# Low parts of the lead's expert blocks made by GpSimd from a copy in SBUF, with a recast selection and an earlier end of the gate steps

## The chip, the cores and the metric

The kernel runs on one core of a Trainium2 chip. The metric is the device time of one execution in microseconds (us), and the profile is one execution taken by the hardware profiler. The core's engines are TensorE (PE, its weight loads PEld), VectorE (DVE), ScalarE (ACT), GpSimd (POOL) and SyncE (SP, which here only issues DMAs). Each runs its own instructions in order and waits for others by semaphores.

## The reference

A block of a transformer with 512 tokens and a model width of 1024: attention and an mLSTM side by side, then a PEER feed-forward. Only the PEER part is touched:

```python
def block(ht):                      # 64 tokens; h: 512 x 1024 in all
    q = (ht @ w_q).reshape(T, PEER_HEADS, 2, PEER_HALF)
    s1 = jnp.einsum('thd,hkd->thk', q[:, :, 0], keys1)
    s2 = jnp.einsum('thd,hkd->thk', q[:, :, 1], keys2)
    v1, i1 = lax.top_k(s1, PEER_TOPK)           # 16 of 128, 8 heads
    v2, i2 = lax.top_k(s2, PEER_TOPK)
    cand = (v1[..., :, None] + v2[..., None, :]).reshape(T, PEER_HEADS, 256)
    cidx = (i1[..., :, None] * PEER_KEYS + i2[..., None, :]).reshape(T, PEER_HEADS, 256)
    top, pos = lax.top_k(cand, PEER_TOPK)
    eidx = jnp.take_along_axis(cidx, pos, axis=-1)
    gate = jax.nn.softmax(top, axis=-1)
    act = gelu(jnp.einsum('thkd,td->thk', u[eidx], ht)) * gate
    return jnp.einsum('thk,thkd->td', act, v[eidx])
```

`u` and `v` have 16384 experts of 1024 numbers each.

## The kernel before

`mix_block` and `query_block` make the attention part and the queries. `peer_block`, which runs from 462.5 us on, is what the change touches. It treats the first 192 tokens and the other 320 differently. For the first 192 it gathers the chosen experts' rows (384 gathers of 128 rows, `pool.indirect_dma_start`, L1428) and DVE takes each with a dot product (`take_row`, L1683) or a scaled addition. For the 320 it computes all 16384 experts densely, in 128 blocks of 128 experts: PE transposes a block of `u`, multiplies it with the tokens, ACT applies the gelu, DVE multiplies with a table of gates that is zero where an expert wasn't chosen, and PE multiplies with the block of `v`.

Products are kept near full precision by splitting an operand in a high part `H` (rounded by ACT) and a low part `L` (what is left), three products in place of one.

**The lead** is the first 56 blocks (`LEAD`). In it only the scores are made and stored to `gelu_table` in DRAM, because the gates don't exist yet. In the same stretch DVE selects the 16 experts of each token and head, for four tiles of 128 tokens one after the other, and PE, DVE and ACT build the gate table in 80 steps (`gates`, `hot_rows`, `stage_gates`): DVE writes one-hot rows, PE multiplies them, ACT copies the result out, SP stores every fifth step's 1280 KB to `gate_table`. A lead block `it` on PE is: transpose block `it+1` to PSUM (`lead_turn`, L1528), 16 matmuls with `H` (L1543), two matmuls that subtract `H` of block `it+1` from its transpose in PSUM (`lead_less`, L1536), 8 matmuls with `L` (L1547), then the block's gate steps (L1555). ACT copies the transpose to `H` (`lead_high`, L1439) and, after L1536, what is left in PSUM to `L` (`lead_low`, L1444).

**What sets the order.** `SEL_AT` says at which block the selection of each of the four tiles must have ended: there DVE ends the softmax (`settle`) and PE turns the choice (`turn_choice`, L1565). The 80 steps are spread over the blocks between these (`gate_steps`), the gathered rows over all turns (`rows_by_turn`; 40 of the 384 in the lead). On DVE, selection code calls `beside(us, cap)`, which counts an estimated clock and puts a lead block's DVE work (`lead_block`: settle, one-hot rows, gathered rows) into the stream when the clock reaches the block's due time (`PE_BLOCK` and `PE_STEP` per block) and the block is before `cap`. After the last selection all remaining lead blocks follow in order. POOL runs only the gathers, six ahead of DVE (`RG`).

**After the lead** come 72 turns with a transpose, scores and values each, then 56 turns with values alone. The seam between lead and turns: SP waits for the last stores of the gate table, loads the first blocks of `v` and then the table's first parts (`load_g`), and DVE's first product with the gates (L1831) waits for these.

Names: `ring` holds loaded blocks of `u`, `peer_psum` is PSUM, `s_all` is a pool of SBUF that holds one-hot rows, selection scratch and later `v`; `s_in` holds candidates during the selection; `stage` holds parts of the gate table; `hT` and `more_rows` the gathered rows.

## Time and profile before

| | us |
|---|---|
| median of 3 runs | 1682.94 (1679.9 to 1685.92) |
| the profiled execution | 1675.21 |
| its span, first to last instruction | 1673.3 |
| PE busy | 1553.4 |
| DVE busy | 1407.6 |
| ACT busy | 618.5 |
| POOL busy | 497.2 |

The profiled execution is 7.7 us shorter than the median of the runs. Where a sum is made against the trace, its result is carried over to the median by the difference that it finds. In the trace the lead lasts from 462.5 us to 840 us, the seam to about 866 us, the 72 turns to 1439 us.

### The profile page before, as it was taken

Reading aid. Unit: us, or ns where it says so; the run is one execution under the profiler, and the core shown is the slowest. Engines: PE = TensorE matmul, PEld = TensorE weight load, DVE = VectorE, ACT = ScalarE, POOL = GpSimd, SP = SyncE. Lnnn points to the kernel's source line nnn. Section 1 sums busy time; section 2 is a strip of 40 time slices with the busy share of each in tenths; the row PEclk is TensorE's granted clock in tenths of the full one; section 3 lists DMA queues with packets and bytes.
Section 4 is the critical chain, followed back from the end, with each engine's and each line's share of the span. In section 5 each row is a group of like instructions: output and inputs, shape, how many; then the busy total and the mean of one; then the engine's idle time right before and its main releaser. Section 6 shows DMA issues by size and latency. Waiting matters only on the chain.

```text
span 1673.3 us, 23249 instructions
## 1 busy us (share of the span) xinstructions
PE 1553.4 (93%) x8386; PEld 1301.7 (78%) x8386; DVE 1407.6 (84%) x3000; ACT 618.5 (37%) x987; POOL 497.2 (30%) x424
## 2 busy tenths in 40 slices
PE   3999988969999689999959999999999999999996
PEld 2454544458899589999959999999999999888884
DVE  5867756649999996859959999999999999988887
ACT  1101423242155345555523333333333333334433
POOL 2000000033201111112235556555555555433330
PEclk8999899979999899999979999999999999999998
DMA  9563021042136556777999999999999999999992
GB/s 354 186 241 144 13 101 51 0 122 87 69 124 220 163 165 203 252 240 255 308 357 381 406 394 398 411 406 391 410 400 400 409 393 402 373 387 378 395 371 108
DMA packets 173425, 454.65 MB, mean 272 GB/s; under 512 B 13768, under 2 KB 72256, under 8 KB 171264
## 3 DMA queue, kind: packets, MB, share of 16 engines
q1 hardware_dynamic: 113152, 234.72, 38.8%
q0 software_dynamic: 59152, 216.07, 33.9%
q10 hardware_dynamic: 1008, 2.38, 0.4%
q8 instruction: 67, 1.10, 0.3%
q14 instruction: 46, 0.38, 0.1%
HBM read 420.58 MB, written 32.24 MB: 271 GB/s over the span
## 4 chain that ended last, share of the span: by engine, by line
PE 59%; DVE 11%; DMA 1%; ACT 1%; issue 1%; DVEq 0%; POOL 0%; ACTq 0%; SPq 0%; POOLq 0%
PE peer_psum L1543 14%; PE peer_psum L1603 7%; PE peer_psum L1614 7%; PE peer_psum L1610 7%; PE peer_psum L1547 7%; PE peer_psum L1555 4%; PE peer_psum L1590 4%; PE peer_psum L1607 4%; PE peer_psum L1616 4%; DVE s_all L1778 2%; DVE s_in L1783 2%; DVE s_all L1781 2%; PE peer_psum L1528 1%; PE peer_psum L1536 1%; DMA stage<-gate_table 1%
## 5 line engine op out<-in xcount | busy, mean ns | idle before, releaser
L1543 PE MATMUL peer_psum<-hH,hi_slots 128*128 128x320 f32 x1024 | 309.3, 316 | 16.9 <-ACT hi_slots L1498 15.4
L1543 PE MATMUL peer_psum<-hL,hi_slots 128*128 128x320 f32 x1024 | 304.0, 310 | 0.0
L1428 POOL DMA_INDIRECT hT<-in_peer_u,eidx x128 | 154.8, 1209 | 326.3 <-DVE dots L1683 277.2
L1464 ACT ACTIVATE hi_slots<-s_all 128x1024 fp32r<-128x1024 f32 x128 | 136.0, 1062 | 206.2 <-PE peer_psum L1616 203.9
L1543 PEld LDWEIGHTS peer_psum<-hH,hi_slots 128*128 128x128 f32 x1024 | 194.2, 190 | 21.9 <-issue 17.8
L1543 PEld LDWEIGHTS peer_psum<-hL,hi_slots 128*128 128x128 f32 x1024 | 194.2, 190 | 2.5
L1428 POOL DMA_INDIRECT hT<-in_peer_v,eidx x128 | 139.0, 1086 | 177.2 <-DVE s_all L1692 166.4
L1812 DVE TENSOR_TENSOR lo_slots<-s_all,hi_slots 128x1024 fp32r<-128x1024 f32 x128 | 156.4, 1222 | 22.9 <-ACT hi_slots L1464 22.9
L1547 PE MATMUL peer_psum<-hH,lo_slots 128*128 128x320 f32 x1024 | 171.7, 310 | 0.0
L1692 DVE SCALAR_TENSOR_TENSOR s_all<-hT,coef,s_all 128x1024 f32<-128x1024 f32 x126 | 161.2, 1279 | 2.5 <-DMA hT<-in_peer_v,eidx 2.1
L1547 PEld LDWEIGHTS peer_psum<-hH,lo_slots 128*128 128x128 f32 x1024 | 158.4, 189 | 4.8
L1603 PE MATMUL peer_psum<-hi_slots,a_hi_lo 128*128 128x512 f32 x512 | 146.7, 408 | 0.0
L1614 PE MATMUL peer_psum<-lo_slots,a_hi_lo 128*128 128x512 f32 x512 | 140.2, 394 | 0.0
L1610 PE MATMUL peer_psum<-hi_slots,a_hi_lo 128*128 128x512 f32 x512 | 139.5, 393 | 0.0
L1452 ACT ACTIVATE s_all<-peer_psum 128x320 f32<-128x320 f32 x128 | 56.0, 437 | 188.3 <-PE peer_psum L1547 182.5
L1610 PEld LDWEIGHTS peer_psum<-hi_slots,a_hi_lo 128*128 128x128 f32 x512 | 99.1, 194 | 20.1
L1614 PEld LDWEIGHTS peer_psum<-lo_slots,a_hi_lo 128*128 128x128 f32 x512 | 98.8, 193 | 20.5
L1495 ACT ACTIVATE a_hi_lo<-s_all 128x320 fp32r<-128x320 f32 x128 | 63.2, 494 | 120.7 <-DVE s_all L1831 120.7
L1428 POOL DMA_INDIRECT more_rows<-in_peer_u,eidx x64 | 72.0, 1126 | 117.9 <-DVE dots L1683 113.1
L1683 DVE CUSTOM_DVE_ANT_0 hT<-hT,h_rows 128x1024 f32<-128x1024 f32 x86 | 104.5, 1219 | 2.2 <-DMA hT<-in_peer_u,eidx 2.0
L1193 POOL TENSOR_TENSOR wqL<-wq,wqH 128x2048 fp32r<-128x2048 f32 x8 | 36.8, 4595 | 233.6 <-ACT wqH L1165 233.6
L1603 PEld LDWEIGHTS peer_psum<-hi_slots,a_hi_lo 128*128 128x128 f32 x512 | 94.1, 195 | 14.9
(305 smaller groups left out, 3042.9 us busy)
## 6 DMA issues: line engine op xcount, KB each, us to landing
ring<-in_peer_u SPq DMA_DIRECT2D x128, 512.0 KB, 7.5
s_all<-in_peer_v SPq DMA_DIRECT2D x128, 512.0 KB, 6.9
gate_table<-stage SPq DMA_DIRECT2D x16, 1280.0 KB, 7.3
stage<-gate_table SPq DMA_DIRECT2D x16, 1280.0 KB, 11.4
x_sb<-in_w_mod POOLq DMA_DIRECT2D x7, 2048.0 KB, 8.7
slab<-in_w_mod SPq DMA_DIRECT2D x5, 2048.0 KB, 15.3
gelu_table<-s_all SPq DMA_DIRECT2D x56, 160.0 KB, 1.9
s_in<-gelu_table SPq DMA_DIRECT2D x56, 160.0 KB, 6.8
```

Of the source, the lines that this page charges most:

```text
L1428: pool.indirect_dma_start(rows_of(j), None, A[table][0], bass.IndirectOffsetOnAxis(eidx[:, k:k + 1], 0)).then_inc(rows_in[j % RG], 16)
L1464: func(H[:, slot_of(w), :], vb[:, w % RING, :], ACT.Copy).then_inc(v_hi, 1)
L1543: mm(ps[:, bank, 0:TD], H[:, b, c * P:(c + 1) * P], h[:, c, T0:T], start=(c == 0 and h is hH), stop=False)
L1547: last = mm(ps[:, bank, 0:TD], L[:, b, c * P:(c + 1) * P], hH[:, c, T0:T], start=False, stop=(c == DC - 1))
L1555: last = mm(ps[:, 6 + m % 2, :].rearrange("p (i t) -> p t i", t=GT)[:, k, :], onehot[:, m % NHOT, k, 0, :], onehot[:, m % NHOT, k, 1, :], ...
L1590: last = tr(ps[:, 6 + (n + half) % 2, c * P:(c + 1) * P], ub[:, n % RING, (4 * half + c) * P:(4 * half + c + 1) * P], ident[:])
L1603: mm(y_bank(g, h), aH[:, NB + g * P:NB + (g + 1) * P], H[:, s, h * 512:(h + 1) * 512], start=first, stop=False)
L1610: mm(y_bank(g, h), aL[:, NB + g * P:NB + (g + 1) * P], H[:, s, h * 512:(h + 1) * 512], start=False, stop=False)
L1614: mm(y_bank(g, h), aH[:, NB + g * P:NB + (g + 1) * P], L[:, s, h * 512:(h + 1) * 512], start=False, stop=final)
L1683: v.tensor_tensor_reduce(out=rows_of(j), in0=rows_of(j), in1=(h_rows if j < K else keep["h_rows_b"])[:], scale=1.0, scalar=0.0, op0=ALU.mu ...
L1692: v.scalar_tensor_tensor(out=y0[:, i, :], in0=rows_of(j), scalar=c, in1=y0[:, i, :], op0=ALU.mult, op1=ALU.add).then_inc(row_done, 1)
L1812: v.tensor_tensor(L[:, s, :], vb[:, w % RING, :], H[:, s, :].bitcast(F32), ALU.subtract).then_inc(v_lo, 1)
```

## The change

- **PE** no longer subtracts. `lead_less` and the constant `minus_one` are gone.
- **ACT** copies the transpose to a new SBUF tile `whole` (one buffer of 128x1024) where it made `L` before. The copy of block `n` waits for GpSimd's subtraction of block `n-1`.
- **POOL** computes `L = whole - H` for each of the 56 lead blocks. The gathers, which POOL issued as early as it could, now stand between the subtractions at places fixed by `ROWS_BY`: six ahead of block 12, five ahead of block 26, then one or two at a block.
- **DVE's selection** adds values and indices in one instruction (tile `pairs`, 16 lists at once) over 11 rectangles, finds the largest of all 8 heads in one pass, and looks up the first 8 of the 16 chosen among the first 20 candidates only. Three groups of three instructions take the place of four.
- **The plan**: `SEL_AT` goes from 10, 20, 32, 45 to 12, 26, 32, 39; the gate steps end at block 50 (`G_END`) in place of 55; of the 40 gathered rows 14 are taken up to block 39 and 26 after (24 and 16 before); DVE's planned clock starts at 11 us.
- **The seam**: SP loads the first part of the gate table and the first four blocks of `v` at lead block 52, in place of after the lead.

```diff
-SEL_AT = {0: 10, 1: 20, 2: 32, 3: 45}
-ROWS_LEAD, ROWS_TAIL = (24, 16), 62
+SEL_AT = {0: 12, 1: 26, 2: 32, 3: 39}
+G_END = LEAD - 6
+DVE_BEHIND = 11.0
+ROWS_LEAD, ROWS_TAIL = (14, 26), 62
...
-    ends = {1: SEL_AT[2], 2: SEL_AT[3], 3: LEAD - 1}
+    ends = {1: SEL_AT[2], 2: SEL_AT[3], 3: G_END}
...
+ROWS_BY = [0 if it < SEL_AT[0] else EIDX_B_AT if it < SEL_AT[1] else RG + sum(ROWS_AT[i] for i in range(it - 2)) for it in range(LEAD)]
...
-RECTS = [(0, 1, 16), (1, 1, 8), (2, 1, 5), (3, 1, 4), (4, 1, 3), (5, 3, 2), (8, 8, 1)]
+RECTS = [(0, 1, 0, 8), (1, 1, 0, 4), (2, 2, 0, 2), (4, 4, 0, 1),
+         (0, 1, 8, 8), (1, 1, 4, 4), (2, 1, 2, 3), (3, 1, 2, 2), (4, 1, 1, 2), (5, 3, 1, 1), (8, 8, 0, 1)]
+FIRST = sum(nr * nb for r, nr, b0, nb in RECTS[:4])
...
+        whole = sb("whole", [P, D])
...
-            sp.wait_ge(g_full, GSTEPS)
-            for w in range(RING):
-                load_v(w)
-            for i in range(2):
-                sp.wait_ge(g_stored[i], 16 * (NTB // 2))
-            for i in range(2):
-                load_g(i)
+                if it == G_END + 2:
+                    for i in range(2):
+                        sp.wait_ge(g_stored[i], 16 * (NTB // 2))
+                    load_g(0)
+                    sp.wait_ge(g_full, GSTEPS)
+                    for w in range(RING):
+                        load_v(w)
+
+            load_g(1)
...
+            issued = 0
+            for n in range(LEAD):
+                b = n % 2
+                while issued < ROWS_BY[n]:
+                    gather(issued)
+                    issued += 1
+                pool.wait_ge(u_copied, n + 1)
+                nc.gpsimd.tensor_tensor(L[:, b, :], whole[:], H[:, b, :].bitcast(F32), ALU.subtract).then_inc(u_low, 1)
+            for j in range(issued, NROWS):
+                gather(j)
...
                 func(H[:, n % 2, :], uT_of(n % 2), ACT.Copy).then_inc(u_high, 1)
-
-            def lead_low(n):
-
-                act.wait_ge(u_less, n + 1)
-                func(L[:, n % 2, :], uT_of(n % 2), ACT.Copy).then_inc(u_low, 1)
+                if n:
+                    act.wait_ge(u_low, n)
+                func(whole[:], uT_of(n % 2), ACT.Copy).then_inc(u_copied, 1)
...
                 if n >= 2:
-                    pe.wait_ge(u_low, n - 1)
+                    pe.wait_ge(u_copied, n - 1)
...
-            def lead_less(n):
-
-                pe.wait_ge(u_high, n + 1)
-                for i in range(2):
-                    last = mm(ps[:, 2 * (n % 2) + i, :], minus_one[:], H[:, n % 2, i * 512:(i + 1) * 512],
-                              start=False, stop=True, skip_group_check=True)
-                last.then_inc(u_less, 1)
...
-            clock, due, blk = 0.0, 0.0, 0
+            clock, due, blk = DVE_BEHIND, 0.0, 0
...
-                for h in range(0, PH, 4):
-                    largest(v, step, [(top[:, t, h + i, :], pos[:, h + i, :], cv[:, h + i, :], work[:, i, :]) for i in range(4)])
-                    beside(4.6, cap)
+                largest(v, step, [(top[:, t, h, :], pos[:, h, :], cv[:, h, :], work[:, h, :]) for h in range(PH)])
+                beside(6.6, cap)
                 step(v.tensor_copy(posf, pos[:]))
-                for h in range(0, PH, 2):
...
+                for h, nh, k, n in ((0, PH, 0, FIRST), (0, 4, 8, NCAND), (4, 4, 8, NCAND)):
+                    hit, us = hit_of(nh, n), 0.18 + nh * 8 * n * 1.04e-3
```

POOL's stream in the lead, before: nothing but gathers after the last subtraction of the query stage (`wqL`).

```order
L1193 TENSOR_TENSOR wqL<-wq,wqH 128x2048 x8
L1412 IOTA iota_i 128x128
L1428 DMA hT<-in_peer_u,eidx 128x1024 x4
L1428 DMA more_rows<-in_peer_u,eidx 128x1024 x2
L1418 DMA eidx<-chosen_u 64x64
```

And after, the first 29 subtractions (`lo_slots` is `L`, `hi_slots` is `H`):

```order
L1447 TENSOR_TENSOR lo_slots<-whole,hi_slots 128x1024 x12
L1437 DMA hT<-in_peer_u,eidx 128x1024 x4
L1437 DMA more_rows<-in_peer_u,eidx 128x1024 x2
L1447 TENSOR_TENSOR lo_slots<-whole,hi_slots 128x1024 x14
L1427 DMA eidx<-chosen_u 64x64
L1437 DMA hT<-in_peer_u,eidx 128x1024 x4
L1437 DMA more_rows<-in_peer_u,eidx 128x1024
L1447 TENSOR_TENSOR lo_slots<-whole,hi_slots 128x1024 x2
```

The gathers have moved behind subtractions, and the subtractions of blocks 12 and 26 behind six and five gathers.

DVE's look-up of a tile's chosen experts, before (each of these groups of three stands four times):

```order
L1775 CAST s_in<-top_pos 128x128
L1778 TENSOR_TENSOR s_all<-iota,s_in 128x1600
L1781 TENSOR_TENSOR s_all<-s_all,s_in 128x1600
L1783 TENSOR_REDUCE s_in<-s_all 128x32
L1778 TENSOR_TENSOR s_all<-iota,s_in 128x1600
```

And after (the second group stands twice):

```order
L1777 CAST s_in<-top_pos 128x128
L1781 TENSOR_TENSOR s_all<-iota,s_in 128x1280
L1783 TENSOR_TENSOR s_all<-s_all,s_in 128x1280
L1785 TENSOR_REDUCE s_in<-s_all 128x8x8
L1781 TENSOR_TENSOR s_all<-iota,s_in 128x1600
L1783 TENSOR_TENSOR s_all<-s_all,s_in 128x1600
L1785 TENSOR_REDUCE s_in<-s_all 128x4x8
```

Three groups, the first of 1280 elements, stand for four of 1600.

SP at the seam, before (the last store of the gate table, then `v`, then both parts of the table):

```order
L1374 DMA gelu_table<-s_all 128x320
L1379 DMA gate_table<-stage 128x16x160
L1363 DMA s_all<-in_peer_v 128x1024 x4
L1366 DMA stage<-gate_table 128x2560 x2
L1360 DMA ring<-in_peer_u 128x1024 x2
```

And after, from the last store of the gate table at block 50 on:

```order
L1385 DMA gate_table<-stage 128x16x160
L1366 DMA ring<-in_peer_u 128x1024
L1380 DMA gelu_table<-s_all 128x320
L1372 DMA stage<-gate_table 128x2560
L1369 DMA s_all<-in_peer_v 128x1024 x4
L1366 DMA ring<-in_peer_u 128x1024
```

The first part of the table and four blocks of `v` are now asked for before the last three lead blocks' loads.

## Rows read from the trace of the kernel before

**Rows 1.** Windows: stretch, length, busy time per engine, granted clock, DMA share, GB/s.
```profile
462.40:565.00 102.60, 101.02 (x707) 98.72 (x708) 99.26 (x361) 57.29 (x69) 10.45 (x11) 1.00 0.55 179
565.00:640.00 75.00, 53.30 (x359) 50.10 (x357) 73.39 (x186) 27.70 (x36) 12.27 (x9) 0.89 0.49 157
...
840.00:880.00 40.00, 22.80 (x128) 21.11 (x129) 21.71 (x37) 8.88 (x16) 12.74 (x12) 0.79 0.99 362
880.00:1430.00 550.00, 549.51 (x3245) 501.08 (x3244) 528.30 (x746) 207.69 (x340) 308.06 (x266) 1.00 1.02 399
```
**Rows 2.** Timeline of PE in the lead: start, duration, line, operation, idle before.
```profile
488.31 0.62 PE L1536 MATMUL peer_psum<-hi_slots,minus_one 128*128 128x512 f32 x2
488.77 1.34 PE L1547 MATMUL peer_psum<-hH,lo_slots 128*128 128x320 f32 x8
...
493.63 1.34 PE L1547 MATMUL peer_psum<-hH,lo_slots 128*128 128x320 f32 x8
...
640.23 1.34 PE L1547 MATMUL peer_psum<-hH,lo_slots 128*128 128x320 f32 x8
...
645.98 1.32 PE L1547 MATMUL peer_psum<-hH,lo_slots 128*128 128x320 f32 x8
```
**Rows 3.** Timeline of DVE, selection of the first tile.
```profile
473.88 0.29 DVE L1758 CAST idxf<-idx 128x256 f32<-128x256 uint32 x1
...
483.86 1.82 DVE L1778 TENSOR_TENSOR s_all<-iota,s_in 128x1600 f32<-128x1600 f32 x1
485.72 1.82 DVE L1781 TENSOR_TENSOR s_all<-s_all,s_in 128x1600 f32<-128x1600 f32 x1
487.58 1.82 DVE L1783 TENSOR_REDUCE s_in<-s_all 128x32 f32<-128x1600 f32 x1
...
506.70 0.29 DVE L1758 CAST idxf<-idx 128x256 f32<-128x256 uint32 x1
```
**Rows 4.** Timeline of DVE: a gate step, a gathered row, the next step.
```profile
670.98 0.68 DVE L1719 TENSOR_TENSOR s_all<-iota,selT 128x512 f32<-128x512 f32 x1
671.58 1.11 DVE L1723 TENSOR_SCALAR s_all<-iota,selT 128x128 f32<-128x128 f32 x4
672.61 1.22 DVE L1683 CUSTOM_DVE_ANT_0 hT<-hT,h_rows 128x1024 f32<-128x1024 f32 x1
...
673.75 0.68 DVE L1719 TENSOR_TENSOR s_all<-iota,selT 128x512 f32<-128x512 f32 x1
```
**Rows 5.** Waits of PE, 462 to 880 us: total, times, longest.
```profile
PE peer_psum L1565 <- DVE gate_b L1704: 16.3, 1, 16.3
```
**Rows 6.** Groups by line: busy, mean ns, idle before.
```profile
L1444 ACT ACTIVATE lo_slots<-peer_psum 128x1024 fp32r<-128x1024 f32 x56 | 57.5, 1026 | 95.7 <-PE peer_psum L1536 95.7
L1193 POOL TENSOR_TENSOR wqL<-wq,wqH 128x2048 fp32r<-128x2048 f32 x8 | 36.8, 4595 | 233.6 <-ACT wqH L1165 233.6
```
**Rows 7.** Single lines' instructions: count, ns min/median/max, first and last start in us.
```profile
L787 DVE TENSOR_SCALAR mod_sum<-slab,cols x5: 486/487/646, 20.7 to 179.2; 128x512 f32<-128x512 f32 x5
...
L789 DVE SCALAR_TENSOR_TENSOR mod_sum<-slab,cols,mod_sum x35: 751/752/1024, 21.2 to 184.4; 128x512 f32<-128x512 f32 x35
...
L379 POOL TENSOR_SCALAR_AFFINE_SELECT x_sb<-x_sb x4: 629/818/1118, 165.6 to 169.6; 128x512 f32<-128x512 f32 x4
...
L1428 POOL DMA_INDIRECT hT<-in_peer_u,eidx x128: 936/946/2547, 506.7 to 1156.4; - x128
```
**Rows 8.** Timeline of the seam: the last gate steps, then who waits for what.
```profile
837.78 2.18 PE L1555 MATMUL peer_psum<-s_all 128*128 128x128 f32 x17
...
861.56 0.49 DVE L1831 TENSOR_TENSOR s_all<-s_all,stage 128x320 f32<-128x320 f32 x1 [13.20 <-DMA stage<-gate_table]
...
863.14 0.61 PE L1543 MATMUL peer_psum<-hH,hi_slots 128*128 128x320 f32 x1 [15.39 <-ACT hi_slots L1498]
```
**Rows 9.** DMA issues: count, KB each, median us to landing.
```profile
gate_table<-stage SPq DMA_DIRECT2D x16, 1280.0 KB, 7.3
stage<-gate_table SPq DMA_DIRECT2D x16, 1280.0 KB, 11.4
```

More of the change, by code:

```diff
@@ L1312, in peer_block @@
         iota = sb("iota", [P, P])
-        minus_one = sb("minus_one", [P, P], F32R)
         stat = sb("y_stat", [P, 5, 8])
@@ L1412, in _, with gather @@
             nc.gpsimd.iota(iota_i[:], pattern=[[1, P]], base=0, channel_multiplier=0).then_inc(iota_ready, 1)
-            pool.wait_ge(eidx_ready, 1)
-            for j in range(NROWS):
+            def gather(j):
+                if j == 0:
+                    pool.wait_ge(eidx_ready, 1)
                 if j == EIDX_B_AT:
@@ L1757, in _ @@
                 cap = SEL_AT[t]
[L1758 to L1760 removed]
+                found = pairs_of[:, 1, :, :]
+                step.put(v.tensor_copy(pairs_of[:, 0, :, :], val[:, t, :, :]))
+                step(v.tensor_copy(found, idx[:, t, :, :]))
```

58 lines of the change are left out of this document (24 added, 34 removed).

## The prediction

> **What bounds the kernel now.** I read the windows by stage first, then the timelines of PE and DVE in the lead, then the waits of PE, and last the seam. [rows 1] show three regimes. Up to 565 us PE is 98% busy and DVE 97%, each with its own work. From 565 to 640 us DVE is 98% busy and PE 71%: PE waits for DVE, with one wait of 16.3 us for the end of a softmax [rows 5] and several short ones, and the granted clock falls to 0.89. From 640 to 840 us PE sets the pace. From 840 to 880 us PE is 57% busy at a granted clock of 0.79, which is the seam. The 72 turns after it run with PE at 100% (549.51 of 550) and DVE at 96%; the change leaves their work alone, so everything is decided before 866 us.
>
> In the lead one block without gate steps takes PE 493.63 - 488.77 = 4.86 us, and one with a single step 645.98 - 640.23 = 5.75, so a step costs 0.9 [rows 2]. 56 x 4.86 + 80 x 0.92 = 346, and 3.5 for the start make 349; the lead lasts 462.5 to 839.9, where the last gate matmul ends [rows 8], 377. So about 28 us of the lead are waits for DVE, nearly all between 565 and 640 us.
>
> **PE's subtraction goes.** L1536 starts 0.46 us before L1547 [rows 2]; with the pipeline's overlap it is worth 0.43 a block, 24 us for 56. A block falls to 4.43. It is a gain only where PE sets the pace.
>
> **DVE's selection gets shorter.** One tile took 506.70 - 473.88 = 32.8 us [rows 3]. The look-up was 4 groups of 3 instructions at a pitch of 1.86, 22.3 us. After it is 2 x 3 x 1.86 = 11.2 and one group of 1280 elements, by proportion 3 x (1.82 x 1280/1600 + 0.04) = 4.5, together 15.7: 6.6 saved. Eight heads in one pass save some four waits of 0.1, and the 11 rectangles with one more copy cost what 14 small additions did. So 26 us a tile, 27.5 for the others with their tail: the four selections would end near 585 us where they ended at about 639, in part because fewer lead blocks are now put among them (the plan puts 2 gathered rows and one softmax there, and all 80 steps and 38 rows behind them).
>
> **ACT** makes `whole` in the time of the old `L`, 1.03 us [rows 6]. It has room: 2.5 us of 4.43 a block.
>
> **POOL's subtraction** is the new cost. 128x2048 took it 4.6 us [rows 6], so 128x1024 takes 2.3 to 2.5; I take 2.4. The path of a block is `H` 1.03, `whole` 1.03, subtraction 2.4, some 4.7 with the semaphores, and PE needs it 6.7 after the transpose (the 4.86 of a block split in that timeline into 0.9 of transpose, 2.3 of `H` matmuls, 0.43 and 1.2 of `L` matmuls: 3.5 for the block's own matmuls, 0.9 for the next transpose, 2.3 for the next `H` matmuls). The path itself is covered. Two places aren't: at block 12 six gathers, 0.95 us each [rows 7] and 0.3 between two, stand in front (PE waits about 5), and at block 26 five gathers that wait for rows DVE has taken. If the cover is gone at every block, the cycle `whole` plus subtraction, 3.6, plus a wait for DVE still lies under 4.43 to 5. In blocks 0 to 25 such waits cost nothing by themselves, since DVE reaches the softmax of tile 1 later than PE block 26 in any case.
>
> **What the subtraction does to DVE** decides the sign. [rows 7]: DVE's L789, with two inputs in SBUF, takes 752 ns, and 1024 in the stretch 165.6 to 170.7 where POOL works on SBUF; POOL's L379 takes 629 alone and 1118 when it starts behind L789; DVE's L787, with one input and a scalar, goes from 487 to 646 beside it; POOL's gathers go from 946 to 2547 behind a long DVE instruction. So they take turns, and one waits until the other is done, with some 0.2 us of overlap on DVE's side and 0.15 on POOL's. The Trainium skill ("SBUF — State Buffer", section "Who interferes with whom") states the same as a rule: a DVE instruction with two SBUF inputs, or in a two-port mode, and a GpSimd instruction that reads SBUF exclude each other for the whole instruction. The page would have the change lose most of what it gains, and the trace agrees as far as these few instructions go. One-input instructions beside POOL's old subtractions show no such growth, so the largest-of passes and reductions hide a part.
>
> Hence a subtraction costs DVE at most 2.4 - 0.35 = 2.05 us. In the selections (474 to 585 us) 25 fall; about half of DVE's time there is in two-input instructions, and a reduction of 1.82 hides most of one: between 0 and 25, taken 17. They end at 602. Behind them DVE has in one row 80 steps at 670.98 to 672.61, 1.63 each = 130; 38 gathered rows at 673.75 - 672.61, 1.14 = 43 [rows 4]; softmaxes and choices 5: 178 us, every instruction of the excluded kinds. Some 29 subtractions fall into it, 29 x 2.05 = 59 (bounds 0 and 65). And one chain of waits, about 11: DVE's row, the fifth gather, subtraction 26, PE's block 26 and its turned choice, then DVE's first step; PE stands still about 20 us before it and its clock will fall as it did before, 1.5 more. 602 + 178 + 59 + 12 = 851. DVE sets this; PE alone (56 x 4.43 + 74 + 3.5 and 15 of waits) would be through at 803. So the lead ends at 851 in place of 840: 11 us lost, with all 24 us of PE's saving off the path.
>
> **The seam.** Before, the last steps end at 840 us, the last store takes 7.3, the load 11.4 [rows 9], DVE waits 13.2 for it and PE 15.4 [rows 8]; with the lower clock the seam costs about 17. After, the steps end five blocks earlier and the load is asked for at block 52, some 15 us before the lead's end. Against a full gain: 1.3 MB of table and 2 MB of `v` come in while `u`, scores and gathers take some 340 GB/s, and the stage tops out near 400 [rows 1]; and POOL, which until then had gathered ahead, is only a row or two ahead at block 55, so that DVE waits for rows in turns 56 and 57. I take 12 of the 17 (bounds 5 and 17). The SP loads of `u` behind them are four blocks ahead and hide a delay of some 10 us.
>
> **Sum**: +11 - 12 - 0.4 (no wait for `minus_one`) = -1, so 1672 to 1673 of span, and 1682.9 - 1, about **1682 us** as a median. The case's own range is 1668 to 1695: 20 subtractions' worth of doubt in the 59 and 17, and the seam's bounds.
>
> **Rivals.**
> - *Little exclusion* (or for two-input instructions alone, not for the one-input steps L1723, which are 60% of a gate step): then the lead ends at 803 to 837 and PE sets the pace. With the seam's 12 to 15, 1631 to 1667. For it: the rows behind the exclusion are other forms than these, a handful; and gathers delay DVE hardly at all. Against it: all of them show it. 1645 as its middle.
> - *More than the full price, the slower side*: POOL's subtraction is longer than half of 4.6 and grows when it alternates with DVE, 2.7 in place of 2.4. At 56 x 0.3 = 17 us on DVE the lead ends at 868 and the kernel takes 1698. It decides from 2.45 us a subtraction on (5 us over the forecast). For it: a fixed part in POOL's 4.6, and L379's four executions with a median of 818 against 629. Against: a wait for DVE is not longer work.
> - *The seam is not hidden*: table and `v` arrive late, or DVE's rows do, and only 5 of 17 are gained: 1690. For it: DMA share 0.99 in the old seam [rows 1].
> - *The change moves PE's wait without shortening anything*: PE, rid of L1536, waits for POOL at each block. This is inside the forecast already, as long as DVE ends later than PE.
>
> **How the numbers follow.** About 0.3%, 5 us, is what a measurement of this kernel can tell from no change: faster is under 1678, slower over 1688. Forecast 0.50, of it 0.16 faster, 0.19 same, 0.15 slower. Little exclusion 0.25, all faster. Full price and more 0.17, slower. Seam not hidden 0.08, slower. Together 0.41 faster, 0.19 same, 0.40 slower. The range 1650 to 1702 leaves out the better half of the first rival and the worst of the second, under 0.2.
>
> **What would show it.** Right: in the lead DVE's L1721, L1725 and L1685 (the old L1719, L1723 and L1683, 0.68, 1.11 for four and 1.22 us [rows 4]) take longer on average, by some 60 us together; POOL's subtraction ranges from 2.4 to over 4; PE waits for DVE through most of the gate steps, with one wait of 15 to 25 us at block 26 for `lo_slots`; the load of the table ends no wait over 3 us. Wrong: DVE's means are unchanged and the lead ends near 803; or the lead ends after 860; or PE still waits over 8 us for `stage` or `s_all` behind it. The forecast falls also if the gathers at block 26 hold PE for 40 us rather than 20, since everything behind it is one chain.

## The result, and the profile after

The changed kernel takes 1703.45 us (median of four runs, 1701.06 to 1709.02) against 1681.42 (1679.01 to 1685.92) for the kernel before on the same chip: a ratio of 1.0133, interval 1.0098 to 1.0167. It is slower by some 22 us. The forecast was 1682, with a range that ended at 1702; both the size and the range missed.

The profiled execution of the changed kernel took 1701.95 us, its span is 1700.2; before, 1675.21 and 1673.3. The 26.9 us between the spans are placed by the times at which blocks end, counted from TensorE's first transpose of the lead (462.9 us before, 459.3 after):

| us | before | after | difference | forecast |
|---|---|---|---|---|
| start of the lead | 462.9 | 459.3 | -3.6 | -0.4 |
| lead: first transpose to its last matmul | 377.1 | 405.5 | +28.4 | +11 |
| from there to the end of block 60 | 53.8 | 49.9 | -3.9 | -12 |
| blocks 61 to 127 | 545.2 | 551.2 | +6.0 | 0 |
| the rest | 234.3 | 234.3 | 0 | 0 |

The lead is 17.4 us worse than forecast and the seam 8.1. The -3.6 lies ahead of anything that the change touches; the +6.0 lies in turns whose work is unchanged. In the twelve executions profiled below that stretch takes 544.6 to 549.7 us whatever was edited (before 545.2), and the two medians are 22.0 apart where the two spans are 26.9 apart. I take most of the +6.0 for spread between executions; nothing here proves it.

The windows of the changed kernel by stage (stretch, length, busy us of PE, PEld, DVE, ACT and POOL with instruction counts, granted clock, DMA share, GB/s) answer to [rows 1]:

```profile
459.30:565.00 105.70, 100.40 (x709) 99.45 (x710) 103.17 (x341) 58.35 (x71) 66.42 (x30) 0.97 0.53 175
565.00:630.00 65.00, 26.78 (x179) 26.43 (x178) 44.84 (x133) 15.69 (x20) 25.27 (x13) 0.68 0.32 100
630.00:760.00 130.00, 117.67 (x885) 112.81 (x883) 126.61 (x280) 70.48 (x101) 46.43 (x23) 1.00 0.66 209
760.00:868.00 108.00, 93.68 (x680) 90.25 (x680) 97.86 (x189) 48.87 (x69) 61.37 (x38) 0.98 0.84 285
868.00:905.00 37.00, 25.81 (x143) 23.99 (x144) 26.57 (x45) 10.50 (x18) 16.32 (x15) 0.82 1.00 387
```

Before, the weak stretch (565 to 640 us) had PE at 71% and DVE at 98%: DVE was the bound. Now, from 565 to 630 us, no engine is even 70% busy: PE 26.78 of 65 us, DVE 44.84, POOL 25.27, and DMA 0.32. The engines wait for one another there, as the waits below show. The granted clock falls to 0.68 there, where it was 0.89. From 630 to 760 us DVE is at 97% and PE at 91%: DVE sets the pace.

DVE's costliest groups in the lead, before (line, operation, output and inputs, shapes, count, then busy us, mean ns, idle before):

```profile
L1723 DVE TENSOR_SCALAR s_all<-iota,selT 128x128 f32<-128x128 f32 x320 | 88.9, 347 | 0.0
L1719 DVE TENSOR_TENSOR s_all<-iota,selT 128x512 f32<-128x512 f32 x80 | 55.0, 688 | 23.7 <-PE peer_psum L1555 23.4
L1778 DVE TENSOR_TENSOR s_all<-iota,s_in 128x1600 f32<-128x1600 f32 x16 | 29.2, 1826 | 0.5
L1783 DVE TENSOR_REDUCE s_in<-s_all 128x32 f32<-128x1600 f32 x16 | 29.1, 1819 | 0.5
```

The same groups after, with one of the gathered rows and POOL's subtraction:

```profile
L1725 DVE TENSOR_SCALAR s_all<-iota,selT 128x128 f32<-128x128 f32 x320 | 137.3, 491 | 0.0
L1721 DVE TENSOR_TENSOR s_all<-iota,selT 128x512 f32<-128x512 f32 x80 | 56.8, 710 | 0.1
L1685 DVE CUSTOM_DVE_ANT_0 hT<-hT,h_rows 128x1024 f32<-128x1024 f32 x26 | 34.6, 1350 | 7.8 <-DMA hT<-in_peer_u,eidx 7.8
L1781 DVE TENSOR_TENSOR s_all<-iota,s_in 128x1600 f32<-128x1600 f32 x8 | 19.3, 2412 | 0.3
L1785 DVE TENSOR_REDUCE s_in<-s_all 128x32 f32<-128x1600 f32 x8 | 14.6, 1820 | 0.3
...
L1447 POOL TENSOR_TENSOR lo_slots<-whole,hi_slots 128x1024 fp32r<-128x1024 f32 x56 | 145.8, 2604 | 167.5 <-ACT whole L1462 167.4
```

The gate steps' 320 scalar instructions grow from 347 to 491 ns on average and from 88.9 to 137.3 us in busy time (consecutive ones overlap in the records, so the busy time is the better measure: 48 us); the two-input ones of 1600 elements from 1826 to 2412; the reduction of the same 1600 elements stays at 1820. One instance in the gate steps, DVE first and then POOL (start, duration, engine, line, operation, idle before):

```profile
644.11 1.11 DVE L1725 TENSOR_SCALAR s_all<-iota,selT 128x128 f32<-128x128 f32 x4
645.14 0.68 DVE L1721 TENSOR_TENSOR s_all<-iota,selT 128x512 f32<-128x512 f32 x1
645.74 3.16 DVE L1725 TENSOR_SCALAR s_all<-iota,selT 128x128 f32<-128x128 f32 x4
648.83 0.68 DVE L1721 TENSOR_TENSOR s_all<-iota,selT 128x512 f32<-128x512 f32 x1
```

```profile
645.24 2.82 POOL L1447 TENSOR_TENSOR lo_slots<-whole,hi_slots 128x1024 fp32r<-128x1024 f32 x1 [4.76 <-ACT whole L1462]
```

Four scalar instructions take 1.11 us alone and 3.16 beside the subtraction: 2.05 more, which is the price that the forecast took from [rows 7].

The longest waits of PE from 455 to 900 us (engine and line, what it waited for, us in total, times, longest), to set against [rows 5]:

```profile
PE peer_psum L1553 <- POOL lo_slots L1447: 43.9, 4, 38.2
PE peer_psum L1561 <- DVE s_all L1725: 18.1, 31, 1.2
PE peer_psum L1549 <- DVE lo_slots L1821: 11.3, 1, 11.3
```

One wait of 38.2 us for POOL, at block 26, where the forecast had about 20. What stands behind it is in the waits of all engines from 575 to 640 us:

```profile
ACT whole L1462 <- POOL lo_slots L1447: 38.4, 1, 38.4
PE peer_psum L1553 <- POOL lo_slots L1447: 38.2, 1, 38.2
POOL hT L1437 <- DVE dots L1685: 32.6, 3, 22.5
DVE chosen_u L1793 <- DMA eidx<-chosen_u: 12.5, 1, 12.5
```

and in POOL's timeline there (columns as above):

```profile
577.38 2.38 POOL L1447 TENSOR_TENSOR lo_slots<-whole,hi_slots 128x1024 fp32r<-128x1024 f32 x1 [2.01 <-ACT whole L1462]
579.71 0.59 POOL L1427 DMA_DIRECT2D eidx<-chosen_u  x1
602.79 2.34 POOL L1437 DMA_INDIRECT hT<-in_peer_u,eidx  x1 [22.49 <-DVE dots L1685]
613.22 0.95 POOL L1437 DMA_INDIRECT hT<-in_peer_u,eidx  x1 [8.09 <-DVE dots L1685]
...
622.29 2.35 POOL L1447 TENSOR_TENSOR lo_slots<-whole,hi_slots 128x1024 fp32r<-128x1024 f32 x1
```

It is a ring of four engines. POOL's copy of tile 1's indices (L1427) stands in its queue behind the 14 subtractions of blocks 12 to 25, so it is issued at 579.71, though DVE has the indices ready at 536.8 (before, they were ready at 540.1 and the copy was issued at 540.3). DVE may not overwrite `chosen_u` until that copy has landed, and stands 12.5 us (L1793). POOL's next gathers wait 22.5, 8.1 and 2.0 us for DVE's rows, which DVE reaches only between parts of its third and fourth selections. The subtraction of block 26 stands behind those gathers, and PE and ACT behind it.

At the seam, ACT is the engine that waits (its timeline; the second line is a wait for the store of the scores):

```profile
860.47 0.44 ACT L1470 ACTIVATE s_all<-peer_psum 128x320 f32<-128x320 f32 x1 [1.58 <-PE peer_psum L1553]
875.20 0.44 ACT L1470 ACTIVATE s_all<-peer_psum 128x320 f32<-128x320 f32 x1 [14.29 <-DMA gelu_table<-s_all]
```

with the DMAs that were asked for around it:

```profile
852.14 0.32 SPq L1380 DMA_DIRECT2D gelu_table<-s_all  x1
852.58 0.36 SPq L1372 DMA_DIRECT2D stage<-gate_table  x1
852.98 2.64 SPq L1369 DMA_DIRECT2D s_all<-in_peer_v  x4
...
856.54 0.33 SPq L1380 DMA_DIRECT2D gelu_table<-s_all  x1
```

The table's load and four blocks of `v`, 3.3 MB, are asked for from 852.58 on, and the store of block 53's scores at 856.54, behind them. ACT may not make the scores of block 55, which reuse that buffer, before this store has landed. The wait for `stage` [rows 8] is gone, and this one stands in its place.

### The profile page after: what moved, and what is told of

The parts are those of the page before. It is cut to its first block, busy times and chain, and to the rows that moved or that the text cites. A ratio compares the mean times of both kernels' runs of the same rounds, so it can differ in the third digit from the quotient of the medians.

```text
span 1700.2 us, 23052 instructions
## 1 busy us (share of the span) xinstructions
PE 1534.1 (90%) x8274; PEld 1283.2 (75%) x8274; DVE 1456.5 (86%) x2980; ACT 612.6 (36%) x986; POOL 643.1 (38%) x480
## 4 chain that ended last, share of the span: by engine, by line
PE 53%; DVE 14%; DMA 3%; POOL 1%; ACT 1%; issue 1%; DVEq 0%; ACTq 0%
PE peer_psum L1549 13%; DVE s_all L1725 7%; PE peer_psum L1553 7%; PE peer_psum L1605 7%; PE peer_psum L1616 7%; PE peer_psum L1612 7%; PE peer_psum L1592 3%; PE peer_psum L1609 3%; PE peer_psum L1618 3%; DVE s_all L1721 3%; PE peer_psum L1542 2%; DVE hT L1685 1%; DMA gelu_table<-s_all 1%; DMA hT<-in_peer_v,eidx 1%; DMA hT<-in_peer_u,eidx 1%
## 5 line engine op out<-in xcount | busy, mean ns | idle before, releaser
L1447 POOL TENSOR_TENSOR lo_slots<-whole,hi_slots 128x1024 fp32r<-128x1024 f32 x56 | 145.8, 2604 | 167.5 <-ACT whole L1462 167.4
L1437 POOL DMA_INDIRECT hT<-in_peer_u,eidx x128 | 151.2, 1181 | 128.5 <-DVE dots L1685 119.4
L1814 DVE TENSOR_TENSOR lo_slots<-s_all,hi_slots 128x1024 fp32r<-128x1024 f32 x128 | 156.5, 1222 | 22.7 <-ACT hi_slots L1482 22.6
L1694 DVE SCALAR_TENSOR_TENSOR s_all<-hT,coef,s_all 128x1024 f32<-128x1024 f32 x126 | 161.3, 1280 | 6.9 <-DMA hT<-in_peer_v,eidx 6.8
L1725 DVE TENSOR_SCALAR s_all<-iota,selT 128x128 f32<-128x128 f32 x320 | 137.3, 491 | 0.0
L1612 PEld LDWEIGHTS peer_psum<-hi_slots,a_hi_lo 128*128 128x128 f32 x512 | 99.1, 193 | 20.1
L1561 PE MATMUL peer_psum<-s_all 128*128 128x128 f32 x640 | 86.6, 283 | 22.2 <-DVE s_all L1725 18.1
```

Of the source, the lines that this page charges most:

```text
L1437: pool.indirect_dma_start(rows_of(j), None, A[table][0], bass.IndirectOffsetOnAxis(eidx[:, k:k + 1], 0)).then_inc(rows_in[j % RG], 16)
L1447: nc.gpsimd.tensor_tensor(L[:, b, :], whole[:], H[:, b, :].bitcast(F32), ALU.subtract).then_inc(u_low, 1)
L1612: mm(y_bank(g, h), aL[:, NB + g * P:NB + (g + 1) * P], H[:, s, h * 512:(h + 1) * 512], start=False, stop=False)
L1694: v.scalar_tensor_tensor(out=y0[:, i, :], in0=rows_of(j), scalar=c, in1=y0[:, i, :], op0=ALU.mult, op1=ALU.add).then_inc(row_done, 1)
L1725: ins = v.tensor_scalar(onehot[:, b, k, 1, :], iota[:], selT[:, 1, d:d + 1], selT[:, 2, d:d + 1], ALU.is_equal, ALU.mult)
L1814: v.tensor_tensor(L[:, s, :], vb[:, w % RING, :], H[:, s, :].bitcast(F32), ALU.subtract).then_inc(v_lo, 1)
```

## The experiments

Four theories stood against one another.

- *Exclusion*: POOL's subtraction and DVE's two-input and scalar instructions keep each other out, for as long as the subtraction lasts. Taking the subtraction off POOL gives the loss back; a subtraction whose result nobody uses takes it again.
- *The path*: the new chain ACT, POOL, PE holds up the blocks by itself, whatever DVE does. Then an unused subtraction costs little.
- *The ring at block 26*: the copy of the indices and the gathers stand in the wrong place of POOL's queue. Moving them gives back the part of the loss that the forecast had not counted.
- *The seam*: the early loads have turned one wait into others. Either the order of the requests does it (store behind loads), and moving the store or spreading the loads pays, or the DMA engines are simply full there, and neither does.

All kernels start from the changed kernel; ratios are to the kernel before on the same chip. "Lead" is the time to block 55's end, 405.5 us in the changed kernel.

**Tile 1's indices copied early.** POOL issues the copy ahead of the subtraction of block 20 in place of block 26.

```
+EIDX_B_IT = 20
-                if j == EIDX_B_AT:
-                    pool.wait_ge(eidx_ready, 2)
-                    pool.dma_start(eidx[NB:P, K:K + KB], chosen_u[0:NB, 0, KB:K]).then_inc(eidx_b_in, 16)
...
             for n in range(LEAD):
+                if n == EIDX_B_IT:
+                    pool.wait_ge(eidx_ready, 2)
+                    pool.dma_start(eidx[NB:P, K:K + KB], chosen_u[0:NB, 0, KB:K]).then_inc(eidx_b_in, 16)
```

> The changed kernel, but GpSimd's small copy of the expert indices of tile 1 (eidx<-chosen_u) is issued before the subtraction of block 20 and not behind that of block 25. Theory A (a ring of waits: DVE's third selection waits 12.5 us for this copy, and everything behind it in the lead hangs on DVE): that wait goes, subtraction 26 and the lead's end come about 12 us earlier, 1691 us. Theory B (the lead is lost to the exclusion between DVE and GpSimd alone, the wait is slack): 1703, within 3 us of the changed kernel.

Measured: 1693.3 us, ratio 1.0084 (1.0053 to 1.0114). DVE's wait of 12.5 is gone; the lead takes 398.4, 7.1 less. PE's wait at block 26:

```profile
PE peer_psum L1553 <- POOL lo_slots L1447: 37.4, 4, 31.9
```

The ring's first link is real, but worth 7 rather than 12. Counted from the lead's start, DVE's third selection ends 8.9 us earlier (117.4 in place of 126.2) and the fourth 6.8 (148.7 in place of 155.5). The missing parts are exclusion that the wait had hidden. Summed over the same instructions, those of the third selection take 3.5 us more than in the changed kernel (one L1769 of 128x64 elements goes from 0.22 to 2.41 us; of the others some gain and some lose), and those of the fourth 2.2 more, nearly all of it in the one-input L1764, which takes 2.37 us for 0.23. An engine that stands still is not slowed by its neighbour.

**And the gathers behind the subtraction of block 26.** The same, with the five gathers due one block later.

```
-ROWS_BY = [... else EIDX_B_AT if it < SEL_AT[1] else ...]
+ROWS_BY = [... else EIDX_B_AT if it <= SEL_AT[1] else ...]
```

> As a1, and the five gathers in front of subtraction 26 are moved behind it. Theory A: PE's wait at block 26 for lo_slots (38 us in the changed kernel) falls under 3 us, PE turns tile 1's choice at once, and DVE doesn't wait 6.4 us for it: another 8 to 12 us under a1, 1680. Theory B: no different from a1.

Measured: 1693.92 us, ratio 1.0086 (1.0053 to 1.0119), the same as with the early copy alone. PE's wait for `lo_slots` at block 26 is gone, and there is another:

```profile
PE peer_psum L1571 <- DVE gate_b L1706: 22.7, 1, 22.7
```

PE now waits for the softmax that DVE makes behind its fourth selection. The lead is 5.6 us shorter in this execution (392.8), which the medians of the runs don't show. The profiled execution loses it elsewhere: its lead starts 1.1 us later than that of the kernel with the early copy alone, and blocks 61 to 127 take 2.9 us more, which is inside the spread of that stretch. So POOL's place in the ring can be taken by DVE itself: whoever is asked, DVE's selections are late.

**The seam as before.** SP asks for `v` and the table behind the lead's last block.

```
-                if it == G_END + 2:
-                    ... (waits for g_stored, load_g(0), wait for g_full, load_v(0..3))
+            sp.wait_ge(g_full, GSTEPS)
+            for w in range(RING):
+                load_v(w)
+            for i in range(2):
+                sp.wait_ge(g_stored[i], 16 * (NTB // 2))
+            for i in range(2):
+                load_g(i)
```

> The changed kernel with SP's loads of the table and of the first v blocks put back behind the lead. Theory C (loading early only exchanges the wait for the table for ACT's wait of 14.3 us for the scores' store that lies behind those loads): the seam costs about 4 us more than now, 1707. Theory D (the early loads hide the seam, and the wait seen has another cause): 12 us or more slower, 1715.

Measured: 1701.91 us, ratio 1.0145 (1.0119 to 1.0171), against 1.0133 with the early loads. The seam from block 55's end to 57's takes 26.6 us in place of 25.5. DVE's wait for the table is back:

```profile
DVE s_all L1832 <- DMA stage<-gate_table: 8.8, 1, 8.8
```

That wait vanishes with the early loads and the time does not. They are worth 1 or 2 us, less than these runs can tell from nothing.

**TensorE makes the low parts, all else as changed.** This undoes the one part that the change is named for: ACT makes `L` from PSUM, PE adds minus `H`; the selection, the plan and the seam stay. POOL's loop over the lead blocks is gone, so its copy of the indices and its gathers are issued as early as before, too.

```
-            for n in range(LEAD):          # POOL
-                pool.wait_ge(u_copied, n + 1)
-                nc.gpsimd.tensor_tensor(L[:, b, :], whole[:], H[:, b, :].bitcast(F32), ALU.subtract).then_inc(u_low, 1)
+            def lead_low(n):               # ACT
+                act.wait_ge(u_copied, n + 1)
+                func(L[:, n % 2, :], uT_of(n % 2), ACT.Copy).then_inc(u_low, 1)
+            def lead_less(n):              # PE
+                pe.wait_ge(u_high, n + 1)
+                for i in range(2):
+                    last = mm(ps[:, 2 * (n % 2) + i, :], whole[:, 0:P].bitcast(F32R), H[:, n % 2, i * 512:(i + 1) * 512], start=False, stop=True, ...)
+                last.then_inc(u_copied, 1)
```

> The changed kernel with the low parts made as before (two matmuls on PE, ACT's copy from PSUM), POOL with the gathers alone; selection, plan and seam as changed. If the exclusion costs DVE what the forecast said, L1725, L1721 and L1685 go back to 347, 688 and 1220 ns, the lead ends some 40 us earlier than in the changed kernel (22 us earlier than in the kernel before) and with 4 us from the seam the kernel takes about 1657 us. If the loss is in the new selection or plan and not in GpSimd's part: 1690 or more.

Measured: 1650.99 us, ratio 0.9848 (0.9819 to 0.9877): faster than both kernels, by 26 us than before. The lead takes 360.7 us, 44.8 less than in the changed kernel, though PE does more work in it. DVE's groups, and PE's two longest waits from 455 to 900 us:

```profile
L1743 DVE TENSOR_SCALAR s_all<-iota,selT 128x128 f32<-128x128 f32 x320 | 88.7, 342 | 0.0
L1703 DVE CUSTOM_DVE_ANT_0 hT<-hT,h_rows 128x1024 f32<-128x1024 f32 x86 | 104.2, 1217 | 8.3 <-DMA hT<-in_peer_u,eidx 8.2
...
PE peer_psum L1548 <- DMA ring<-in_peer_u: 3.9, 1, 3.9
PE peer_psum L1563 <- DVE lo_slots L1839: 3.8, 1, 3.8
```

The scalar instructions are back at 342 ns and PE hardly waits at all. So the selection, the plan and the seam are worth 26 us together, and the subtraction on POOL costs 48 (1.0133 - 0.9848 of 1680), with what it does to POOL's queue. How much of that is the queue, the two edits before tell: with the early copy the kernel is still 42.3 us slower than this one on the same chip, and with the gathers moved as well 42.9.

Set against this kernel, the changed one's 44.8 us in the lead fall apart by stage. DVE's four selections end 155.5 us after the lead's start and not 120.7, which is 34.8 more: 12.5 are the wait for the copy, and 22.3 are longer instructions, since DVE has no other wait in them that this kernel lacks. From DVE's copy of the first turned choice to the last gate matmul it is 214.6 us for 196.5, 18.1 more. Behind the last gate step 7.3 come back, 22.0 for 29.3. DVE's steps alone take 48 us more behind the selections, but only 18 of them show: without the subtraction PE sets the pace of that stretch (192.57 us busy of 197, DVE 167.14), with it DVE does (211.57 of 215). The 24 us that the change takes off PE are inside these figures. What they would bring without exclusion no run shows.

**The same, with an unused subtraction on POOL.** It has the size and the place of the changed kernel's (once a block, gathers around it as there), reads two other tiles and writes one that nobody reads. Nothing waits for it but POOL's own queue.

```
+                pool.wait_ge(u_high, n + 1)
+                nc.gpsimd.tensor_tensor(scratch[:], gg2[:, 0:W_IDLE], x_sb[:, 0, 0:W_IDLE], ALU.subtract).then_inc(idle_done, 1)
+                pool.wait_ge(idle_done, n + 1)
```

> a4 (low parts by PE and ACT again) plus one GpSimd subtraction of 128x1024 from SBUF at each lead block, at the places of the changed kernel, whose result nobody reads. Theory E (the exclusion itself slows DVE): L1725's counterpart back to about 490 ns, gathered rows to about 1.35 us, DVE sets the lead again, and the kernel takes a4 + 30, about 1681 us. Theory F (the loss is the path: PE and ACT waiting for GpSimd's result): within 5 us of a4.

Measured: 1706.68 us, ratio 1.0181 (1.0155 to 1.0207), as slow as the changed kernel or slower; the lead takes 410.7 us.

```profile
L1451 POOL TENSOR_TENSOR scratch<-gg,x_sb 128x1024 f32<-128x1024 f32 x56 | 147.9, 2641 | 169.9 <-ACT hi_slots L1464 169.4
L1748 DVE TENSOR_SCALAR s_all<-iota,selT 128x128 f32<-128x128 f32 x320 | 142.0, 504 | 0.0
L1708 DVE CUSTOM_DVE_ANT_0 hT<-hT,h_rows 128x1024 f32<-128x1024 f32 x86 | 109.5, 1280 | 12.1 <-DMA hT<-in_peer_u,eidx 12.1
```

Scalar instructions are at 504 ns again. The path through POOL's result is therefore not the cause: a subtraction that nobody waits for costs all of it, 56 us against the kernel without it, where 30 were expected. This part holds what POOL does to DVE and what it does to POOL's own queue: DVE's wait of 12.4 us for the copy of the indices is here too, and PE waits 28.6 us for the softmax behind the selections. PE makes the low parts itself here, by the forecast 24 us of work, and the lead is only 5.2 us longer than the changed kernel's: that saving is nearly all off the path.

**The same, with writes only.** Three memsets of 128x1024 a block in place of the subtraction.

```
+                for i in range(3):
+                    nc.gpsimd.memset(scratch[:], 0.0).then_inc(idle_done, 1)
+                    pool.wait_ge(idle_done, 3 * n + i + 1)
```

> As b1, with three memsets of 128x1024 in place of the subtraction: GpSimd writes SBUF and reads nothing. If two-input instructions of DVE meet GpSimd on its reads alone, as the Trainium skill has it (SBUF — State Buffer, section Who interferes with whom), the two-input instructions (one-hot of 128x512, gathered rows) stay at 688 and 1220 ns, and the one-input steps (128x128 TENSOR_SCALAR), if they run in a two-port mode, still grow. If any GpSimd access excludes all of them: all three grow.

Measured, in one execution: 1681.88 us; the lead takes 386.4. DVE's groups and its longest wait:

```profile
L1452 POOL MEMSET scratch<- 128x1024 f32 x168 | 163.4, 973 | 129.2 <-ACT hi_slots L1465 122.4
L1749 DVE TENSOR_SCALAR s_all<-iota,selT 128x128 f32<-128x128 f32 x320 | 117.6, 512 | 0.0
L1709 DVE CUSTOM_DVE_ANT_0 hT<-hT,h_rows 128x1024 f32<-128x1024 f32 x86 | 104.2, 1218 | 15.5 <-DMA hT<-in_peer_u,eidx 15.4
...
DVE chosen_u L1817 <- DMA eidx<-chosen_u: 26.4, 1, 26.4
```

The rows, with two inputs, are not touched (1218 ns for 1217) while POOL is busy for longer than with its subtractions. The scalar instructions are delayed all the same: 117.6 us busy for 88.7, 29 us more. The lead is 25.7 us longer than without the memsets, but that is not the price of these 29. DVE waits 26.4 us for the copy of the indices, which stands behind the memsets of 26 blocks, and its selections end 158.7 us after the lead's start for 120.7; from the first turned choice to the last gate matmul it is 197.7 us for 196.5, since PE sets the pace there (193.41 us busy of 198). So two kinds of exclusion show: a write on POOL stops DVE's one-input scalar form, and only a POOL instruction that also reads stops DVE's two-input ones. The Trainium skill ("SBUF — State Buffer", section "Who interferes with whom") states just this split, and both halves agree with these rows.

**Half a subtraction.** POOL subtracts 512 of 1024 columns; the other half of `L` is made zero once ahead of the lead and stays so, which means that this kernel leaves out that half of the low part in the `u` scores.

```
-                nc.gpsimd.tensor_tensor(L[:, b, :], whole[:], H[:, b, :].bitcast(F32), ALU.subtract).then_inc(u_low, 1)
+                nc.gpsimd.tensor_tensor(L[:, b, 0:512], whole[:, 0:512], H[:, b, 0:512].bitcast(F32), ALU.subtract).then_inc(u_low, 1)
```

> The changed kernel with GpSimd's subtraction on 512 of the 1024 columns; the other half of the low parts is zero, so the u scores of the lead leave out that part. If the loss is the time for which the subtraction holds the port (2.35 us at 1024 columns), DVE's growth (46 us on L1725, 6 on L1685 and 7 to 10 on the look-up) halves and the kernel is 20 to 28 us faster than the changed one, about the time of the kernel before. If it is a price per instruction: within 5 us of the changed kernel.

Measured: 1677.65 us, ratio 1.0001 (0.9979 to 1.0024); the lead takes 377.6, 27.9 less.

```profile
L1730 DVE TENSOR_SCALAR s_all<-iota,selT 128x128 f32<-128x128 f32 x320 | 111.0, 407 | 0.0
L1452 POOL TENSOR_TENSOR lo_slots<-whole,hi_slots 128x512 fp32r<-128x512 f32 x56 | 79.4, 1418 | 203.7 <-ACT whole L1467 203.6
```

What the scalar instructions have over their 88.7 us falls from 48.6 to 22.3 as POOL's instruction falls from 2604 to 1418 ns: the price goes by the time that POOL holds on, with no large fixed part. PE's wait at block 26 is still 33.8 us, though, and DVE's wait for the copy of the indices has grown from 12.5 to 19.9: the copy comes 117.0 us after the lead's start (120.4 in the changed kernel), and the sooner DVE's selections are there, the longer they wait. So the ring and the exclusion are two things, and each hides a part of the other.

**The scores' store from ACT's queue at the seam.** For blocks 50 to 55.

```
-                sp.dma_start(S_dram[it], act_out[:, it % 2, :]).then_inc(s_stored[it % 2], 16)
+                if it < G_END:
+                    sp.dma_start(...)
...
+                if it >= G_END:
+                    act.wait_ge(s_ready, it + 1)
+                    nc.scalar.dma_start(S_dram[it], act_out[:, it % 2, :]).then_inc(s_stored[it % 2], 16)
```

> The changed kernel, the scores of blocks 50 to 55 stored from ACT's DMA queue and not from SP's. Theory G (the store of block 54 lies behind 3.3 MB of loads in SP's queue, and ACT's gelu of block 56 waits 14.3 us for it): that wait falls under 5 us and the kernel is 9 us faster than the changed one, 1691 us at the chip of the first four experiments. Theory H (the DMA engines are full, whichever queue): the wait stays over 10 us, no gain over 3 us.

Measured: 1700.54 us, ratio 1.0148 (1.0121 to 1.0176). ACT's wait shrinks and DVE's grows, from 10.2 us in the changed kernel (waits from 838 to 905 us):

```profile
DVE hT L1689 <- DMA hT<-in_peer_u,eidx: 17.0, 8, 6.4
...
ACT s_all L1471 <- DMA gelu_table<-s_all: 4.8, 1, 4.8
```

Blocks 55 to 57 take 18.9 us, 6.6 less, and 57 to 60 take 28.0, 3.6 more.

**`v` spread over the last blocks.** One block of `v` asked for per turn in place of four at once.

```
-                    for w in range(RING):
-                        load_v(w)
+                if it >= G_END + 2:
+                    load_v(it - G_END - 2)
```

> The changed kernel, with the table's first part asked for at block 52 as it is and the four blocks of v one at a time at blocks 52 to 55. Theory G: fewer bytes ahead of the store of block 54 (2.3 MB for 3.3), some 4 us of ACT's 14.3 us wait go, 1696 us. Theory H: no gain.

Measured: 1699.06 us, ratio 1.0124 (1.0096 to 1.0152). Blocks 55 to 57 in 18.3 us, 57 to 60 in 29.9, 5.5 more. Each edit takes 7 us off the place it aims at and half or more comes back within three blocks. The DMA share is 1.00 in the changed kernel (868 to 905 us), 1.02 with the stores moved (866 to 905) and 1.03 with `v` spread (870 to 905). That speaks for full DMA engines and against the order of the requests as the main cause, and neither kernel differs measurably from the changed one.

**Combinations.** TensorE's low parts with each form of the seam, to see whether the seam matters more when the lead is quick. With `v` spread:

> a4 with the first four blocks of v asked for one at a time at blocks 52 to 55. In a4 the seam (end of block 55 to end of block 57) takes 18.5 us where 14 are work; if the bytes ahead of the scores' stores make the rest, 2 to 4 us less than a4, 1648 us; if the DMA engines are full, as a5 and a6 say, within 2 us of a4.

1647.83 us, ratio 0.982 (0.9787 to 0.9853). With the scores stored by ACT:

> a4 with the scores of blocks 50 to 55 stored from ACT's queue. As c1: 2 to 4 us less than a4, or no difference if the DMA engines are full.

1645.9 us, ratio 0.9818 (0.9785 to 0.9852). With the seam of before:

> a4 with the loads of the table and of v behind the lead, as in the kernel before. The gate steps still end at block 50, so the stores are done by then: the wait for the load of the table (11.4 us) stays. If the early loads are worth what a4's seam shows against before's 29.5 us without gate steps, 10 us slower than a4; if they only exchange one wait for another, as a3 against the changed kernel (1 us), within 3 us of a4.

1653.44 us, ratio 0.9839 (0.9799 to 0.9878). From block 55 to 57 they take 12.8, 14.8 and 21.9 us, where TensorE's low parts alone have 18.5. The traces tell the seams apart by up to 9 us; the times do not, since all four intervals overlap. The best of them, 1645.9, is 31 us faster than the kernel before on its chip, and 26 of that come with TensorE's low parts alone.

## Why the prediction was wrong

Where it was right, by its own steps:

- **Exclusion and its price.** It took 2.05 us for a full meeting, and one meeting in the trace shows 3.16 - 1.11 = 2.05. It forecast 59 us behind the selections; DVE's groups show 48 for the scalar forms, 2 for L1721 and 6 for the rows, 56 together, if their durations before are taken as undisturbed. That one-input scalar instructions are excluded as well, the doubt behind the rival *little exclusion*, is settled by the unused subtraction and by the memsets.
- **PE's 24 us are off the path.** With the unused subtraction PE does that work again. The lead is 5.2 us longer than the changed kernel's and the time some 8 (1.0181 for 1.0133, intervals that overlap).
- **The selections without exclusion.** The forecast had all four end at 585, which is 122.5 us after the lead's start. TensorE's low parts show 120.7.
- **From the first gate step of tile 1 on.** The forecast had 851 - 614 = 237 us from there to the lead's end. Measured: 459.3 + 405.5 - 627.9 = 236.9. The agreement is partly luck. The forecast let DVE set all of it, and DVE's steps are through at 842.8, 214.9 us after the first; the last 22.0 us are PE's blocks without steps.
- **The chain from DVE's row to its first step**: 615.9 to 627.9, 12.0 for "about 11".

**The steps that failed in the lead** are the end of the selections and the wait at block 26. The forecast had the selections end at 602 and the first gate step at 614; counted on its scale (the lead starts 3.6 us earlier here) they end at 618.3 and 631.5. Two things make the 16.3 us: a wait of 12.5, and 22.3 of exclusion where 17 were taken, less the 1.8 by which the selections alone are shorter than forecast.

The first is a wait that the forecast doesn't have: 12.5 us in which DVE stands for POOL's copy of the indices. The forecast wrote that the subtraction of block 26 stands behind five gathers, and let the gathers cost PE about 20 us. It did not ask what else had been moved past the subtractions. The copy of the indices, one short DMA, had only gathers beside it in the queue before and stands behind 26 subtractions after, and DVE may not reuse its buffer until the copy lands. The order for this stood in POOL's queue. PE's wait at block 26 came to 38.2 us for about 20.

The second is the term "between 0 and 25, taken 17" for the exclusion in the selections. Measured against TensorE's low parts it is 155.5 - 120.7 - 12.5 = 22.3 us in the changed kernel, where the wait hides a part of it. With the early copy nothing hides it, and it is 148.7 - 120.7 = 28.0, above the forecast's own upper bound. In the changed kernel's fourth selection, with POOL's subtractions held up behind their gathers, DVE's instructions take no longer than with TensorE's low parts.

So of the 17.4 us that the lead is over the forecast, the early copy gives 7.1 back, and what it leaves is near the 28.0 - 17 = 11 of the mis-sized term. The second queue edit shows that with no gathers ahead of block 26 PE still waits 22.7 us for DVE's softmax, a wait that the kernel with TensorE's low parts doesn't have. The forecast's last sentence on signs named the place and the number, PE held "for 40 us rather than 20", but not the cause, and it carried no chance of its own; its other sign of being wrong, a lead that ends after 860, came out as well (864.8).

**The step that failed at the seam** is "I take 12 of the 17": 4 were gained. The mechanism was right as far as it went, and the sign that the text named (no wait over 3 us for the table's load) came out as said. It counted the full DMA engines against a full gain and made them too small: here a hidden load did not shorten the stretch. The loads of `v` and the table push the scores' store back, ACT waits 14.3 us for it, and when that is mended DVE waits for its rows. The rival *seam not hidden* had the size (5 of 17) and gave it 0.08. Even the 4 are mostly not the early loads': with the seam of before the stretch from block 55's end to 60's takes 51.0 us, against 49.9 with them and 53.8 in the kernel before.

**The sum.** +11 and -12 were to cancel. They came out as +28 and -4. Both misses go the same way. The range said to be the case's own, 1668 to 1695, doesn't follow from its parts: the upper bounds of 25 for 17, 65 for 59 and 5 for 12 add 8, 6 and 7 to 1682 and give 1703. That this is near the time measured is luck: the 59 came out at 56, and a wait that no part holds came on top. The rival *more than full price* (2.7 us a subtraction, 1698) was nearest in its time; its mechanism was not: POOL's mean is 2604 ns, but the median is 2474, the shortest 2347 and the longest 3882, so the long ones take turns with DVE, as its counter-argument said. (Its threshold is a slip: 56 x 0.05 us is 2.8 and not 5, so it would decide from 2.5 us on.)

## What to carry to other kernels

Elementwise work moved from a busy engine to GpSimd can be paid by VectorE. Here it was, wherever VectorE ran two-input or scalar forms on SBUF beside it, at 2.05 us for a full meeting with a subtraction that takes 2.35 at its shortest; reductions paid nothing. Where VectorE sets the pace, that is the first term of the sum, ahead of what the relieved engine saves. When instructions are put into an in-order queue, list every short one that ends up behind them, index copies and stores too, and ask whose buffer each of them frees: one such copy, held behind the work of 26 blocks, kept VectorE waiting 12.5, 19.9 and 26.4 us in three of these kernels, the longer the less exclusion there was. In this seam, with the DMA engines full, asking for the loads earlier did not shorten the stretch; the wait came back at whatever was asked for next.

## What the runs showed of the hardware

- **Writes alone are enough to stop the scalar form.** Memsets of 0.97 us raise the busy time of VectorE's 128x128 scalar instructions from 88.7 to 117.6 us, and leave the two-input rows at 1218 ns (1217 without).
- **Short one-input operations are hit like long ones.** In the selection of the early-copy kernel a 128x128 scalar operation of 0.23 us takes 2.37 beside a subtraction: it pays 2.14 us, nine times its own length.
- **Gathers wait for VectorE instructions with two inputs in SBUF.** POOL's gather at 616.17 us takes 1.68 us for the 0.94 of one alone: VectorE's row from 615.81 runs to 617.03, and the gather ends 0.82 behind it. The gather at 602.79 takes 2.34 and ends 0.88 behind L1783, which runs from 602.44 to 604.26. In the kernel before, 71 gathers start beside the 128x1024 subtraction of L1812, and their median is 1.68 us, 0.81 longer than what was left of it; 61 start beside L1838, which has one input in PSUM, and 2 beside a 128x1600 reduction, and these have a median of 0.94:

```profile
602.44 1.82 DVE L1783 TENSOR_TENSOR s_all<-s_all,s_in 128x1600 f32<-128x1600 f32 x1
...
615.81 1.22 DVE L1685 CUSTOM_DVE_ANT_0 hT<-hT,h_rows 128x1024 f32<-128x1024 f32 x1
```

```profile
616.17 1.68 POOL L1437 DMA_INDIRECT hT<-in_peer_u,eidx  x1 [1.99 <-DVE dots L1685]
```

What stays open: the 6 us of blocks 61 to 127 in the profiled execution, what the 24 us saved on PE would bring without the exclusion, whether the 2.9 us that the later gathers lose in blocks 61 to 127 are more than spread, and whether gathers and subtractions could be laid out so that the ring closes nowhere. That last was not tried, since TensorE's low parts are faster by more than the ring costs.
